# Three score and probability buffers instead of two in a dilated attention core (Trainium2, one core)

## What is computed

```python
ATT_HEAD_DIM, ATT_HEADS_PER_GROUP = 64, 8
ATT_PATTERNS = ((128, 1), (512, 4), (2048, 16))     # window, dilation
def _dilated_window_attention(q, k, v, window, dilation):
    ...
    scores = jnp.einsum('brnqhd,brnkhd->brnhqk', q_r, k_b) * (ATT_HEAD_DIM ** -0.5)
    ...
    scores = jnp.where(valid[None, None, :, None], scores, NEG_INF_2)
    m = jnp.max(scores, -1)
    p = jnp.exp(scores - m[..., None])
    l = jnp.sum(p, -1)
    o = jnp.einsum('brnhqk,brnkhd->brnqhd', p, v_b) / l_t[..., None]
...
wgt = l * jnp.exp(m - jnp.max(m, 0, keepdims=True))
merged = jnp.sum(wgt[..., None] * o, 0) / jnp.sum(wgt, 0)[..., None]
```

## Time and profile before

| | us |
|---|---|
| median of 3 runs (4588.47, 4608.1, 4616.5) | 4608.1 |
| profiled execution, its own time | 4618.23 |
| its span, first to last instruction | 4616.5 |
| the stage `att_core` in it, about | 195 |
| TensorE busy in the span | 3881.0 |
| mean granted TensorE clock, share of full speed | 0.916 |

### The profile page before, as it was taken

One profiled execution on the slowest core, in us unless ns is written; L12 is line 12 of the kernel. 1 busy time (PEld: TensorE's weight loads), 2 busy tenths in 40 slices (PEclk: granted clock), 3 DMA queues, 4 the chain that ended last, 5 costly groups with the idle time before them and its releaser, 6 DMA issues. The chain is left out here.

```text
span 4616.5 us, 60235 instructions
## 1 busy us (share of the span) xinstructions
PE 3881.0 (84%) x24648; PEld 2655.3 (58%) x24648; DVE 1724.7 (37%) x3138; ACT 696.0 (15%) x1494; POOL 820.2 (18%) x667
## 2 busy tenths in 40 slices
PE   4989979999998879999999895777749978578773
PEld 2478866884446756874458744444429955444441
DVE  6667746630465654211441612000052344200003
ACT  1212111110222221000211500000020132000000
POOL 1122213430110214420100201000033342100001
PEclk9989979999899989999999997999969987798997
DMA  3221313633121012221121026999932200799995
GB/s 121 73 83 48 121 54 107 224 132 113 29 64 55 2 42 73 82 105 64 57 73 57 1 82 271 397 395 396 399 135 76 72 1 19 297 398 401 401 399 212
DMA packets 252617, 707.63 MB, mean 153 GB/s; under 512 B 22412, under 2 KB 136660, under 8 KB 201716
## 3 DMA queue, kind: packets, MB, share of 16 engines
q1 hardware_dynamic: 234916, 662.10, 39.0%
q10 hardware_dynamic: 12880, 25.72, 1.5%
q0 software_dynamic: 4608, 16.78, 0.9%
HBM read 667.31 MB, written 37.24 MB: 153 GB/s over the span
## 5 line engine op out<-in xcount | busy, mean ns | idle before, releaser
L3247 PE MATMUL experts_pg<-moe_wg,experts_xt 128*64 128x256 f32 x4224 | 523.4, 411 | 129.6 <-DMA moe_wg<-in_moe_w_up 108.1
L3247 PEld LDWEIGHTS experts_pg<-moe_wg,experts_xt 128*64 128x64 f32 x4224 | 330.4, 148 | 305.6 <-issue 159.3
L3262 PE MATMUL experts_py<-moe_wd,experts_ht 128*64 128x512 f32 x1056 | 269.8, 657 | 41.6 <-DVE experts_ht L3314 24.2
L565 PE MATMUL ffn_out_y<-ffn_out_ring,ffn_h 128*128 128x512 f32 x640 | 276.0, 592 | 0.0
L3312 DVE TENSOR_TENSOR experts_h<-experts_hs,experts_pg 128x256 f32<-128x256 f32 x66 | 27.8, 421 | 640.5 <-ACT experts_hs L3281 640.5
L644 PE MATMUL ffn_in_seven<-ffn_in_seven_t,ffn_in_seven_s 128*128 128x256 f32 x1056 | 236.0, 380 | 0.0
L3343 POOL DMA_INDIRECT merge_yg<-y_rows,moe_yi x16 | 15.4, 962 | 1145.8 <-PEq L3330 584.7
L644 PEld LDWEIGHTS ffn_in_seven<-ffn_in_seven_t,ffn_in_seven_s 128*128 128x128 f32 x1056 | 201.6, 191 | 27.8
L565 PEld LDWEIGHTS ffn_out_y<-ffn_out_ring,ffn_h 128*128 128x128 f32 x640 | 121.1, 190 | 151.7 <-issue 150.2
L3262 PEld LDWEIGHTS experts_py<-moe_wd,experts_ht 128*64 128x64 f32 x1056 | 84.9, 149 | 180.9 <-issue 180.9
L3308 DVE COPY experts_xt<-experts_px 128x512 f32<-128x512 f32 x66 | 45.6, 691 | 342.1 <-PE experts_px L3239 342.1
(11 more groups left out here) (720 smaller groups left out, 6726.0 us busy)
## 6 DMA issues: line engine op xcount, KB each, us to landing
moe_wg<-in_moe_w_gate SPq DMA_DIRECT2D x66, 2048.0 KB, 20.5
moe_wg<-in_moe_w_up SPq DMA_DIRECT2D x66, 2048.0 KB, 25.0
moe_wd<-in_moe_w_down SPq DMA_DIRECT2D x66, 2048.0 KB, 26.1
ffn_in_ring<-in_ffn_w_in SPq DMA_DIRECT2D x42, 1024.0 KB, 5.3
ffn_in_ada_ring<-in_ada_w SPq DMA_DIRECT2D x28, 1024.0 KB, 7.3
ffn_out_ring<-in_ffn_w_out SPq DMA_DIRECT2D x20, 1024.0 KB, 5.0
ssd_proj_ring<-in_ssd_w_in SPq DMA_DIRECT2D x19, 1024.0 KB, 5.4
att_kqt<-in_attn_w_qkv SPq DMA_DIRECT2D x17, 1024.0 KB, 5.1
```

What stands on the lines that cost most here:

```text
L565: last = nc.tensor.matmul(y[:, tt, half, :], h[:, kk, tt * P:(tt + 1) * P], ring[n][:, q, half * BANK:(half + 1) * BANK], start=(kk == 0), ...
L3247: last = nc.tensor.matmul(pg[ch * SLOTS:(ch + 1) * SLOTS, b, side, 0:HH], xt[:, b, kk % MQ, kk // MQ, :], wg[:, b, side, kk, ch * HH:(ch + ...
L3262: last = nc.tensor.matmul(py[half * SLOTS:(half + 1) * SLOTS, b, :], ht[:, b, kk % HM, kk // HM, :], wd[:, b, kk, half * HALF:(half + 1) * ...
```

## The change

The tiles `s` and `pr` and the four small ones of row maxima and sums get three buffers (`DEEP`) instead of two. Scores are issued three items ahead instead of two, exponents two ahead instead of one, and the waits on a buffer's last user are moved by one item to match. `psc`, `pt` and `pso` keep two buffers, `pst` one. The list of inverse_sum stays one item ahead of the loop. The instructions of every engine are the same in kind and number.

```diff
+            DEEP = 3
-            s_ = st.sb("s", [P, 2, KEYS])
-            pr = st.sb("pr", [P, 2, KEYS])
+            s_ = st.sb("s", [P, DEEP, KEYS])
+            pr = st.sb("pr", [P, DEEP, KEYS])
...
-            top, ntop, l, rl = (st.sb(n, [P, 2]) for n in ("top", "ntop", "l", "rl"))
+            top, ntop, l, rl = (st.sb(n, [P, DEEP]) for n in ("top", "ntop", "l", "rl"))
...
-                    scores(0)
-                    scores(1)
+                    for n in range(DEEP):
+                        scores(n)
                     turn_probs(0)
                     for n in range(ITEMS):
...
-                        if n + 2 < ITEMS:
-                            scores(n + 2)
+                        if n + DEEP < ITEMS:
+                            scores(n + DEEP)
                         if n + 1 < ITEMS:
                             turn_probs(n + 1)
...
-                        if n >= 2:
-                            act.wait_ge(s["t_made"], n - 1)
+                        if n >= DEEP:
+                            act.wait_ge(s["t_made"], n - DEEP + 1)
...
-                    exponents(0)
+                    for n in range(DEEP - 1):
+                        exponents(n)
                     for n in range(ITEMS):
-                        if n + 1 < ITEMS:
-                            exponents(n + 1)
+                        if n + DEEP - 1 < ITEMS:
+                            exponents(n + DEEP - 1)
                         take_turned(n)
...
                         dve.wait_ge(s["s_made"], n + 1)
-                        if n >= 2:
-                            dve.wait_ge(s["exp_done"], n - 1)
+                        if n >= DEEP:
+                            dve.wait_ge(s["exp_done"], n - DEEP + 1)
...
                         dve.wait_ge(s["exp_done"], n + 1)
-                        if n >= 2:
-                            dve.wait_ge(s["norm_done"], n - 1)
+                        if n >= DEEP:
+                            dve.wait_ge(s["norm_done"], n - DEEP + 1)
...
-                    first(0)
-                    first(1)
+                    for n in range(DEEP):
+                        first(n)
                     inverse_sum(0)
                     for n in range(ITEMS):
                         if n + 1 < ITEMS:
                             inverse_sum(n + 1)
-                        if n + 2 < ITEMS:
-                            first(n + 2)
+                        if n + DEEP < ITEMS:
+                            first(n + DEEP)
                         if n >= 2 and n % 2 == 0:
                             take_pair(n - 1)
```

More of the change, by code:

```diff
@@ L2874, in _ @@
                     for n in range(ITEMS):
-                        b = n % 2
+                        b = n % DEEP
                         pool.wait_ge(s["inv_done"], n + 1)
@@ L2895, in turn_probs @@
                         for m in range(6):
-                            last = nc.tensor.transpose(pst[:, m // 4, (m % 4) * P:(m % 4 + 1) * P], pr[:, n % 2, m * P:(m + 1) * P], k.ident[:, :])
+                            last = nc.tensor.transpose(pst[:, m // 4, (m % 4) * P:(m % 4 + 1) * P], pr[:, n % DEEP, m * P:(m + 1) * P], k.ident[:, :])
                         last.then_inc(s["t_made"], 1)
-                    scores(0)
-                    scores(1)
+                    for n in range(DEEP):
+                        scores(n)
                     turn_probs(0)
@@ L2950, in first @@
                     def first(n):
-                        r, h, b = n // H, n % H, n % 2
+                        r, b, d = n // H, n % 2, n % DEEP
                         dve.wait_ge(s["s_made"], n + 1)
-                        if n >= 2:
-                            dve.wait_ge(s["exp_done"], n - 1)
-                        step(nc.vector.tensor_tensor(s_[:, b, 0:T], psc[:, b, 0, :], m0[:, r, :, :].rearrange("p a b -> p (a b)"), ALU.add))
-                        nc.vector.tensor_tensor(s_[:, b, T:KEYS], psc[:, b, 1, 0:2 * P], m12[:, :, :].rearrange("p a b -> p (a b)"), ALU.add).then_inc(s["s_taken"], 1)
+                        if n >= DEEP:
+                            dve.wait_ge(s["exp_done"], n - DEEP + 1)
+                        step(nc.vector.tensor_tensor(s_[:, d, 0:T], psc[:, b, 0, :], m0[:, r, :, :].rearrange("p a b -> p (a b)"), ALU.add))
+                        nc.vector.tensor_tensor(s_[:, d, T:KEYS], psc[:, b, 1, 0:2 * P], m12[:, :, :].rearrange("p a b -> p (a b)"), ALU.add).then_inc(s["s_taken"], 1)
                         dve.wait_ge(s["s_taken"], n + 1)
-                        step(nc.vector.tensor_reduce(top[:, b:b + 1], s_[:, b, :], AX.X, ALU.max))
-                        nc.vector.tensor_scalar(ntop[:, b:b + 1], top[:, b:b + 1], -SCALE, None, ALU.mult).then_inc(s["max_done"], 1)
+                        step(nc.vector.tensor_reduce(top[:, d:d + 1], s_[:, d, :], AX.X, ALU.max))
+                        nc.vector.tensor_scalar(ntop[:, d:d + 1], top[:, d:d + 1], -SCALE, None, ALU.mult).then_inc(s["max_done"], 1)
                     def inverse_sum(n):
-                        b = n % 2
+                        d = n % DEEP
                         dve.wait_ge(s["exp_done"], n + 1)
-                        if n >= 2:
-                            dve.wait_ge(s["norm_done"], n - 1)
-                        nc.vector.reciprocal(rl[:, b:b + 1], l[:, b:b + 1]).then_inc(s["inv_done"], 1)
+                        if n >= DEEP:
+                            dve.wait_ge(s["norm_done"], n - DEEP + 1)
+                        nc.vector.reciprocal(rl[:, d:d + 1], l[:, d:d + 1]).then_inc(s["inv_done"], 1)
                     def take_pair(n):
```

## The result

The changed kernel takes 4579.5 us in the median (4567.5 to 4581.9, five runs), the kernel before 4608.1; the ratio of the runs is 0.9935, with a 95% interval of 0.9912 to 0.9957. By the ratio that is 30 us less (20 to 40 by the interval), where 7 were forecast. It lies inside the forecast range and under the 1% bound, but it is four times the forecast gain.

A forecast was written before the change was run, and what follows sets the result against it. The stage was taken as bound by a chain per item at full clock and by TensorE at half clock. Terms of -9.5 and +2.3 us gave -7, from 4608.1 to 4601 us, range 4576 to 4620.

The forecast's parts named there:

- What bounds the stage: Edited stage, some 195 us: TensorE's work, the chain per item or half clock sets the pace; savings reach the end.
- The chain behind first(m+1): Reciprocal waits behind the next item's first() on VectorE: full-clock items go from 4.90 to 4.5 us, gain 9.5 in all.
- The start: A third first() ahead of the first reciprocal on VectorE shifts all later work: +2.3 us.
- ScalarE's copies as the next bound: Turned copies behind the exponents on ScalarE are ready 4.25 us after the scores, under the chain's 4.98.
- Why more distance helps: Two buffers let TensorE put only one other item's work beside the 6.04 us chain, leaving a 2.21 us standstill.
- The clock term: In the edited stage, half clock keeps its 40% share of time, 72 us before; no gain was counted from it.
- the 7.08: Us between two turns of probabilities at half clock, where the chain is hidden; claimed to stay, with no gain.
- the second rival: Less TensorE idle time makes half clock rarer in the stage: 4588 us, or 4575 if all goes; chance 0.17.
- the sum of -7: Whole program: -9.5 us from the chain per item and +2.3 from the start; this forecast had chance 0.55.

The follow-up runs named there:

- inverse_earlier: The changed kernel with inverse_sum two items ahead of the loop instead of one, ScalarE's list as it was: 4557.7 us, ratio 0.9905.
- two_bufs_new_order: The changed kernel's lists, but two buffers instead of three for scores, probabilities and the small tiles: 4581.1 us, ratio 0.9953.
- slow_norm_after: The changed kernel with an unread 1024-column memset on GpSimd ahead of every norm: ratio 0.9972, about 4601 us.
- filler_before: The kernel before with four unread 128-column products per item on TensorE, between scores and turn: 4589.6 us, ratio 0.9961.

## Why the prediction was right, and where not

- **What bounds the stage**, and that a saving reaches the end: right. The stage is 30 us shorter and the program 30 us faster.
- **The chain behind first(m+1)**: right, in place and nearly in size, 4.43 us per item against 4.5 and a stated 4.37 to 4.58. The wait is 1.27 on every second item in the second part of the stage (1.2 to 1.6 forecast), and spread over nearly all items at the same pace in the first, which was not foreseen. inverse_earlier confirms the cause: with the reciprocal back behind its own first() those waits are gone.
- **The start**: right. The first turn at 16.8 instead of 14.5, and 14.6 when the reciprocal is put back.
- **ScalarE's copies as the next bound**: right, 4.36 against 4.25.
- **Why more distance helps**: the prediction ascribed it to the buffers ("With two buffers TensorE can put only one other item's..."). two_bufs_new_order shows the same gain with two. What limited the item was how far ahead the lists issue scores. By the list, first(n+3) stands behind inverse_sum(n+1) and so behind exponents(n+1), which frees the scores' buffer that it would take of two. And exponents(n+2) can start 2.47 us after the end of their scores (3763.99 to 3766.46), while the turn that frees their buffer of two is done 2.09 after it even with its wait (1.28 + 0.81).
- **The clock term**: this is the step that failed. The sum kept "the share of *time* at half clock" at 40%. It was 16% and 24% (clock 0.92 and 0.88). That takes the time at half clock from 72 us to a mean of 30. Nor did the 7.08 stay: in the changed kernel's two traces no two turns stand that far apart; half clock comes in shorter pieces there, and two items with one of them take 10.2 to 10.5 us instead of 8.86.

  The turns give the sum. The 31 steps from the first turn to the last take 174.8 us in both traces before, and 143.6 and 148.2 after; at 4.90 and 4.43 each they would take 151.9 and 137.3. So the pace gave 14.6 (9.5 forecast, for fewer items), the clock 22.9 less a mean of 8.6, 14.3 (nothing forecast), and the end 1.5, from the last turn to the last copy, which was not in the sum. With 2.3 more at the start that is -28, what the stage measured (194.6 to a mean of 166.5).

  So what came true is the second rival, which had a chance of 0.17. That the time still lies in the range is no merit of the sum of -7: the range was drawn down to the far end of this rival. The reason against it, that the clock stays at half without any idle time, shows that it can stay down without waits, not what brings it down. (The far end of this rival, 4575, is 33 us below and so lies within the 46 us of 1%, unlike what the prediction says.) slow_norm_after and filler_before show it from both sides: waits of up to 2.06 put into the new lists give 0.79, waits filled in the old lists give 0.96.

The time of slow_norm_after, 13 us under the kernel before at an equal stage, stays unexplained.

## What to carry to other kernels

When engines run fixed lists, ask of each wait whether it is for room or for an instruction that stands too far back in its engine's list; the test is to change the lists and leave the tiles as they were. After a step is issued further ahead, every step behind it on the same list has to move with it: here the reciprocal was left behind, and moving it and the copies took the gain from 30 to 52 us by the ratios. And where the trace shows the clock going up and down, as in this one stage, don't price TensorE's recurring waits at their length alone: the share of half clock is a term that can move with them, and unused products in the waits are a test of it.

## What was not expected of the hardware

- Adding 256 passes of unused products to a stage made it 20 us shorter (194.6 to 174.7), with the mean granted clock from 0.80 to 0.96.
- In this stage, with the same matmuls each time, recurring waits of at most 2.06 to 2.22 us went with granted clocks of 0.79 and 0.80 (three traces), of at most 1.28 with 0.88 to 0.92 (four traces), and of 0.57 or none with 0.96 and 0.97 (four traces), where only the first items behind the start are at half clock.
- A short VectorE instruction behind another can start before the first one's recorded end: behind the copy of 0.37 us the next started 0.22 us after its start.
